# Conditioning rows of a decoder trunk through device memory instead of broadcast matmuls

## The reference

```python
c_act = jax.nn.silu(c)
for l in range(DEPTH):
    ada = (c_act @ ada_w[l] + ada_b[l])[:, None, :]
    sh1, sc1, g1, sh2, sc2, g2 = jnp.split(ada, 6, axis=-1)
    h = rms_norm(x, norm_mix_g[l]) * (1.0 + sc1) + sh1
    x = x + g1 * hybrid_mixer(h, ...)     # 8 heads: attention, pooling, recurrence, then w_out
    h = rms_norm(x, norm_ffn_g[l]) * (1.0 + sc2) + sh2
    x = x + g2 * peer_ffn(h, ...)         # 8 heads x 16 experts gathered for every token
return rms_norm(x, final_g)
```

## Time and profile before

| | |
|---|---|
| median of three runs | 2143.58 us |
| lowest, highest | 2141.44, 2143.63 us |
| span of the profiled execution | 2140.2 us |
| PE, PE weight loads | 1886.5 us (88%), 1105.7 us (52%) |
| DVE, ACT, POOL | 1485.8 (69%), 689.8 (32%), 629.5 us (29%) |
| moved by DMA | 713.13 MB, of it 536.90 MB gathers |

### The profile page before, as it was taken

One profiled execution on the slowest core, in us unless ns is written; L12 is line 12 of the kernel. 1 busy time (PEld: TensorE's weight loads), 2 busy tenths in 40 slices (PEclk: granted clock), 3 DMA queues, 4 the chain that ended last, 5 costly groups with the idle time before them and its releaser, 6 DMA issues.

```text
span 2140.2 us, 22226 instructions
## 1 busy us (share of the span) xinstructions
PE 1886.5 (88%) x6428; PEld 1105.7 (52%) x6428; DVE 1485.8 (69%) x4081; ACT 689.8 (32%) x1923; POOL 629.5 (29%) x608
## 2 busy tenths in 40 slices
PE   4999999989889889888799999999989889888777
PEld 3677777654334334333267777775434334334332
DVE  6587687686776766766646676677776766766774
ACT  1222232233333333333322232242333333333332
POOL 4000000044444444444400000002444444445442
PEclk9999999999999999999999999999999999999989
DMA  9855563389999999999986544336999999999997
GB/s 374 327 187 195 213 228 133 124 359 396 426 427 426 427 426 426 427 413 413 424 336 236 201 183 175 128 128 255 386 427 426 428 426 426 426 427 425 408 416 294
DMA packets 118819, 713.13 MB, mean 333 GB/s; under 512 B 13104, under 2 KB 17456, under 8 KB 51120
## 3 DMA queue, kind: packets, MB, share of 16 engines
q0 software_dynamic: 73728, 536.90, 60.0%
q1 hardware_dynamic: 44976, 174.97, 21.8%
HBM read 710.78 MB, written 1.05 MB: 333 GB/s over the span
## 4 chain that ended last, share of the span: by engine, by line
PE 57%; DMA 21%; DVE 12%; ACT 3%; issue 3%; POOL 2%; SPq 2%; DVEq 0%; POOLq 0%; ACTq 0%
DMA wall<-in_peer_uv,idx 19%; PE PS L1239 18%; PE PS L975 11%; PE PS L980 10%; DVE wall L1308 6%; PE PS L985 5%; PE PS L995 3%; POOL wall L634 2%; PE PS L1213 2%; ACT M L853 1%; PE PS L1022 1%; PE PS L1172 1%; ACT wgt L846 1%; DVE pos L1818 1%; PE PS L946 1%
## 5 line engine op out<-in xcount | busy, mean ns | idle before, releaser
L1239 PE MATMUL PS<-wall,M 128*128 128x512 f32 x2032 | 956.3, 621 | 207.1 <-ACT M L853 206.9
L1308 DVE CUSTOM_DVE_ANT_0 wall<-wall,tok 128x1024 f32<-128x1024 f32 x512 | 604.9, 1224 | 337.0 <-DMA wall<-in_peer_uv,idx 337.0
L634 POOL DMA_INDIRECT wall<-in_peer_uv,idx x512 | 570.5, 1114 | 699.9 <-PE PS L1239 512.0
L1239 PEld LDWEIGHTS PS<-wall,M 128*128 128x128 f32 x2032 | 387.7, 198 | 735.7 <-issue 414.4
L839 ACT ACTIVATE dg<-dg 128x2 f32<-128x2 f32 x254 | 51.7, 203 | 751.5 <-DVE dg L1308 751.5
L975 PE MATMUL PS<-hT,wall 128*128 128x256 f32 x1120 | 247.9, 381 | 1.7 <-DMA wall<-in_w_in 1.7
L975 PEld LDWEIGHTS PS<-hT,wall 128*128 128x128 f32 x1120 | 212.1, 190 | 31.4 <-ACT M L717 2.1
L576 POOL TENSOR_SCALAR rsb<-ms 128x4 f32<-128x4 f32 (+2 forms) x22 | 6.2, 284 | 749.8 <-DVE ms L1308 748.5
L980 PE MATMUL PS<-wall,hT 128*128 128x512 f32 x512 | 224.7, 593 | 0.2 <-ACT M L703 0.2
L853 ACT ACTIVATE M<-turn,wgt 128x128 f32<-128x128 f32 x508 | 176.2, 394 | 23.5
L980 PEld LDWEIGHTS PS<-wall,hT 128*128 128x128 f32 x512 | 96.3, 191 | 109.0 <-issue 108.3
(11 more groups left out here) (290 smaller groups left out, 1894.4 us busy)
## 6 DMA issues: line engine op xcount, KB each, us to landing
wall<-in_w_in SPq DMA_DIRECT2D x112, 704.0 KB, 9.6
braw<-in_ada_rows SPq DMA_DIRECT2D x72, 512.0 KB, 4.3
wall<-in_w_out SPq DMA_DIRECT2D x2, 4096.0 KB, 14.8
wall<-in_peer_uv,idx POOLq DMA_INDIRECT x512, 12.3
wall<-in_ada_rows SPq DMA_DIRECT2D x6, 1024.0 KB, 12.2
wall<-in_w_in SPq DMA_DIRECT2D x16, 384.0 KB, 10.1
mix<-in_peer_w_query SPq DMA_DIRECT2D x6, 1024.0 KB, 4.8
wall<-in_w_in SPq DMA_DIRECT2D x16, 320.0 KB, 8.9
```

What stands on the lines that cost most here:

```text
L634: nc.gpsimd.indirect_dma_start(out=pair_rows[b][s], out_offset=None, in_=uv_rows, in_offset=bass.IndirectOffsetOnAxis(ap=idx[i % 2][:, k:k ...
L1239: ins = mm(bank(B_ACC + 2 * t + hf), diag[:, b, s, :], pair_rows[b][s][:, D + hf * 512:D + (hf + 1) * 512], start=(i == FIRST_TILE[t] and ...
L1308: return v.tensor_tensor_reduce(out=o, in0=a, in1=b, scale=1.0, scalar=0.0, op0=ALU.mult, op1=ALU.add, accum_out=acc)
```

## The change

All 32 columns of a layer (24 of the looped heads, 8 of g2) are now kept in one array `acol` [128, 32], which `fold_cols` writes directly. In head 6's step PE turns the array with one matmul into 32 rows of 128 in PSUM, DVE copies them to `arow`, SP stores them to a 16 KB buffer in device memory, waits for the store, and reads them back with a broadcast over all 128 partitions into `ada` (16 KB a partition, 2 MB). `update_first` waits for that read. `block_row`, `block_out`, `gate_rows` and the copies of g2 are gone. The loop's constant `MIX_CHAIN` counts DVE's chained instructions, eight fewer for a pair of heads.

```diff
+ROWS = 4 * KC
-MIX_CHAIN = (160, 158)
+MIX_CHAIN = (152, 150)
-        acol = sb("acol", [P, 3 * KC])
+        acol = sb("acol", [P, ROWS])
+        arow = part(P)
+        bounce = nc.dram_tensor("bounce", (DEPTH, ROWS, P), F32, kind="Internal").ap()
@@ SP, after the loop of a layer
                 load_wq(l, 0, s_r[1])
+                sp.wait_ge(s_rowed, l + 1)
+                sp.dma_start(bounce[l], arow[0:ROWS, :]).then_inc(s_bounce, 16)
+                sp.wait_ge(s_bounce, 16 * (l + 1))
+                sp.dma_start(ada[:].rearrange("p a n -> p (a n)"), brow(bounce[l].rearrange("r n -> (r n)"), 4 * D)).then_inc(s_rows, 16)
                 sp.wait_ge(s_z, UNITS * HEADS * (l + 1))
                 load_wq(l, HEADS - 2, s_ahead)
@@ PE
-                def block_row(m, jm, p, dst):
-
-                    pe.wait_ge(s_col, m * 2 + (2 * H0 + G2_BLOCKS + p + 1))
-                    for i in range(2):
-                        mm(dst[:, i * P:(i + 1) * P], ccol[:, jm, p, i:i + 1].to_broadcast([P, P]), ident[:],
-                           start=True, stop=True)
+                def turn_columns():
+
+                    pe.wait_ge(s_col, (G2_BLOCKS + 2 * (HEADS - 2)) * (l + 1))
+                    mm(bank(B_S1)[0:ROWS, 384:512], acol[:], ident[:], start=True, stop=True)
@@ PE, step
-                    if rows:
-                        block_row(m, jm, 0, bank(B_S1)[:, 256:512])
+                    if isinstance(m, int):
+                        turn_columns()
                     attend(m, jm)
                     pe.wait_ge(s_AH, m + (H0 + 1))
-                    if rows:
-                        block_row(m, jm, 1, bank(B_O)[:, 256:512])
                     recur(m, jm)
@@ PE, first group of the experts
                         key_scores(1)
-                        gate_rows()
@@ DVE
-                def block_out(h, jm, p, src):
-
-                    ch(copy(acol[:, bass.ds(h * 4 + p * 2, 2)], ccol[:, jm, p, :]))
-                    ch(copy(ada[:].rearrange("p a n -> p (a n)")[:, bass.ds(h * 512 + p * 256, 256)], src))
-                        fold_cols(ecol[:, i, :], layer, j, 2).then_inc(s_col, 1)
+                        fold_cols(ecol[:, i, :], layer, j, 2, acol[:, 3 * KC + 2 * i:3 * KC + 2 * i + 2]).then_inc(s_col, 1)
-                        fold_cols(ccol[:, jm, p, :], l, j, 2).then_inc(s_col, 1)
+                        fold_cols(ccol[:, jm, p, :], l, j, 2, acol[:, bass.ds(h * 4 + p * 2, 2)]).then_inc(s_col, 1)
@@ DVE, step and last_pair
                     attended(h)
-                    block_out(h, j, 0, bank(B_S1)[:, 256:512])
                     forget(h + 1, 1 - j)
                     recurred(h)
-                    block_out(h, j, 1, bank(B_O)[:, 256:512])
                     recurred(h)
+                    copy(arow[0:ROWS, :], bank(B_S1)[0:ROWS, 384:512]).then_inc(s_rowed, 1)
                     squares()
@@ DVE, update_first and the first group of the experts
+                    dve.wait_ge(s_rows, 16 * (l + 1))
-                        dve.wait_ge(s_g2, l + 1)
-                        for hf in range(2):
-                            ch(copy(ada[:, 3, hf * 512:(hf + 1) * 512], bank(B_G2[hf])))
```

More of the change, by code:

```diff
@@ L76 @@
 B_H = ((B_S0, B_LA), (2, B_LB))
-B_G2 = (B_S0, B_O)
 B_TURN = (B_S0, B_LA, B_O)
@@ L308, in build @@
         s_pexp = sem("s_pexp")
-        s_g2 = sem("s_g2")
+        s_rowed, s_bounce, s_rows = sem("s_rowed"), sem("s_bounce"), sem("s_rows")
         s_six, s_seven, s_six_rest, s_y_rest = sem("s_six"), sem("s_seven"), sem("s_six_rest"), sem("s_y_rest")
@@ L1070, in step @@
                     jn = 1 - jm
-                    rows = not isinstance(m, int)
                     project(n, jn, 0)
@@ L1256, in expert_rows @@
                                 ins.then_inc((s_half, s_vacc)[hf], 1)
[L1258 to L1265, removed]
                 for g in range(LGROUPS):
@@ L1367, in constants, with fold_cols @@
                 ch.sync()
-            def fold_cols(a, l, j, n):
+            def fold_cols(a, l, j, n, to=None):
                 ch(v.tensor_tensor(a, a, bcol[:, l, bass.ds(j, n)], ALU.add))
                 ch.sync()
-                return v.tensor_tensor(a, a, gcol[:, l, bass.ds(j, n)], ALU.mult)
+                return v.tensor_tensor(a if to is None else to, a, gcol[:, l, bass.ds(j, n)], ALU.mult)
             def scale_rows(t):
```

## The result

The change makes the kernel slower: 2156.31 us against 2143.61 us for the kernel before, run beside it, a ratio of 1.0061 [1.0047, 1.0075]. The forecast was 2131.6 us, 0.56% less. The profiled execution of after took 2151.57 us, with a span of 2149.8 us.

The account below looks back on a forecast made before the run. PE's instruction stream bounds the mixer loops, DMA nearly all the expert stage. Span 2140.2 - 10.8 + 0.45 - 1.6 - 0 = 2128.2 us; with 3.4 around it, 2131.6 us, 0.56% less, range 2127.5 to 2137.

Parts of the forecast that it names:

- rival 1: Expert stage: removing the gate rows gains nothing, because DMA ends last or ACT is late; 2133.2 us, chance 22%.
- The loops, -10.8 us: Mixer loops: conditioning matmuls leave PE's stream, 0.90 us in each of twelve looped heads, paid back in full.
- rival 3: Mixer loops: PE meets a wait of 0.9 us a head, for AH or weights; 2142.4 us, no change, chance 5%.
- The turn, +0.45: Head 6's step: one added matmul before attend, 0.22 us a layer on PE's path; bounds nothing and 0.45.
- The round trip, 0: Head 6 to DVE's gate-row product: store and broadcast read, likely 11 us, worst 23, hidden under 35 us of cover.
- Rival 4: The round trip outlasts its 35 us cover, each further microsecond costing two; 2151.6 us at 45 us, chance 2%.
- The gate rows, -1.6 and 0: Expert stage's start: without sixteen matmul records (1.79 us) the second sum starts 1.6 us sooner in layer 0, 0 in layer 1.
- The earlier gathers find idle DMA: Layer 0's expert stage: DMA share 0.77 from 480 to 490 us leaves idle time for gathers that start sooner.
- The clock: Expert stages' starts: PE's clock left unchanged in the sum, +-3.1 us in the range; one fall more or fewer, chance 21%.

Follow-up runs that it names:

- e_before_off32: The kernel before with 32 unused bytes a partition in front of the SBUF tensor wall (target of mixer weights and gathers): 2165.73 us, ratio 1.0103.
- f_after_aligned: The changed kernel with 224 unused bytes a partition in front of wall, which then begins on a multiple of 256: 2128.25 us, ratio 0.9939 to before.
- a_again: The changed kernel run once more without an edit, beside the kernel before on the same chip: 2153.53 us, ratio 1.0048.
- l_thrice: f_after_aligned with the round trip made three times in series in each layer: 2132.36 us, ratio 0.9956 to before.
- n: f_after_aligned with 32 unused bytes behind wall, so wall stays aligned and the large tensors behind it lie 32 bytes off: 2132.22 us, ratio 0.9953 to before.
- j_all_aligned: The changed kernel with seven small tensors declared elsewhere, so every large SBUF tensor begins on a multiple of 256, without unused bytes: 2131.77 us, ratio 0.9948 to before.
- p_loop_only: The kernel before without the loops' conditioning matmuls and their copies, wall unmoved, g1 set to zero, no round trip: 2135.39 us, ratio 0.9962 to before.
- k_gate_back: f_after_aligned with the gate rows of g2 made by matmuls again in each layer: 2134.77 us, ratio 0.9963 to before.
- c_out: The changed kernel with the round trip through the first 32 KB of the output tensor and no internal tensor: 2153.85 us, ratio 1.0046 to before.

## Why the prediction was wrong

**The step that failed** is a term that the prediction's sum doesn't have. Its parts go through the matmuls, the copies, the round trip, the queue and the clock, and none takes a price for the declaration `acol = sb("acol", [P, ROWS])` or names it. It stands in the diff as plainly as the matmuls. Its price is the largest of all: e_before_off32 makes this edit's shift alone and takes 2165.73 - 2142.61 = 23.1 us; between f_after_aligned and a_again, with the change in both and each beside before on its own chip, the ratios differ by 0.0109, 23.3 us. The second half of the same failure is in rival 1, "DMA, whose bytes are fixed, is what ends last in the expert stage". The bytes are fixed. The rate was taken as fixed with them, and it fell from 427 to 417 GB/s. The size fits: the gathers' 8 KB packets together took 1278.9 us of 16 engines in before and 1299.2 in after, 20.3 us more, and the two expert stages are 9.9 and 9.7 us longer.

With `wall` aligned, four kernels that leave PE's stream as the change has it gave 0.9939 (f_after_aligned), 0.9956 (l), 0.9953 (n) and 0.9948 (j). The forecast was 2131.6/2143.58 = 0.9944. So the sum of the parts that were costed came out, and the error is the one part that was not. Some of the closeness is luck. The profiled executions of these four have spans 15.0, 12.7, 8.9 and 10.2 us under before's, where the sum had 12.0; in f_after_aligned the turn and a wait in layer 1 cost more than was taken, and the clock and a microsecond before head 2 gave more. The points, with the landmarks of f_after_aligned (head 2's step at 162.96, first gather 426.29, second sum 446.51, last sum 1071.02, output projection's end 1458.96, second sum of layer 1 at 1484.65, end 2125.2):

- **The loops, -10.8 us.** Right as a step: 164.28 to 207.37 is 43.09 us in after, against 43.98, and 43.09 in f_after_aligned too. In one of the twelve it isn't whole. Layer 1's first step in after is 1127.45 to 1171.41, still 43.96 us, since DVE waits for the rows of `ada_w` for 8.66 us inside it and PE then waits for DVE. In f_after_aligned that step is 1114.56 to 1157.96, 43.40 us. That is rival 3, with DMA as the late one, for 0.3 to 0.9 us in all. End to end p_loop_only gives 8.1 us [5.1, 10.9] for the loops, so the 10.8 stand as steps and are not shown to arrive in full.
- **The turn, +0.45.** Too small. Head 6's step is 340.08 to 383.69, 43.61 us, against 43.08: 0.53 us a layer, 1.06 in all, above the worst that was taken, 0.45 a layer. The matmul and the one behind it show as two pieces where the prediction took one of 0.22:

```profile
374.92 0.34 PE PS L1045 x2
375.25 0.42 PE PS L1050 x2
```

- **The round trip, 0.** Right, and its parts too: 1.4 and 7.3 us where 2 and 8 were taken, with 4 and 18 as the worst. DVE's product is still released by PE (at 410.85 in after). Rival 4, in which the round trip outlasts its cover, is refuted: one takes 8.7 us, and three in l_thrice still fit. The cover of 35 us measured as 32 to 33 (377.46 to 410.85 in after).
- **The gate rows, -1.6 and 0.** The sizes are right; in layer 0 the reason is only half of it. From the first gather to the second sum, before takes 455.60 - 433.78 = 21.8 us, after 20.2 and f_after_aligned 20.2. In layer 1, from the end of the output projection to the second sum, before takes 25.65 us (1474.28 to 1499.93), after 25.68 (1474.12 to 1499.80), f_after_aligned 25.69. ACT is late next, as said. What the prediction didn't say is that the rows cost something only behind a first sum at the lower clock. In the profiles of after and f_after_aligned that sum ran at the full clock (3.70 us), where the rows would have cost nothing (above), so their 1.6 us against before can't be told from a clock that didn't fall. That the rows' removal gives the time where the clock does fall is seen in j_all_aligned: 5.20 us for the first sum and still 20.2.
- **The earlier gathers find idle DMA.** From 480 to 490 us before moved 285 GB/s. After moves 411, which is all that it can at its rate, f_after_aligned 424 and k_gate_back 353; but c_out, with the schedule of after, moves 336. The profiled stage of f_after_aligned, 446.51 to 1071.02, is 1.7 us shorter than that of before.
- **The clock.** Layer 0's fall at the narrow matmuls is shorter, 5.24 us for the eight records in after and f_after_aligned (before 6.61), and layer 1 has a fall in after (5.24) that before (3.54) and f_after_aligned (3.54) don't have; k_gate_back had 6.39 in layer 0, l_thrice 3.54. It isn't the change that decides: a_again is after without an edit and had 6.41 where after had 5.24, and 5.22 for its first expert sum where after had 3.70. The same kernel falls or not from execution to execution, by up to 3 us at a place, and p_loop_only shows three slower places in one execution where the prediction's range allowed for one.

For one profile of each the differences between f_after_aligned and before add up: -7.5 up to the first gather (5.4 of the loop, less 0.5 for the turn, 1.4 of the clock, and about 1 before head 2 that no edit explains), -1.6 at the gate rows, -1.7 in the stage, -4.5 in the second mixer (five steps of 0.89, one of 0.58, less 0.5), +0.3 in the last stage: -15.0, the difference of the spans.

## What to carry to other kernels

Before costing the work that a change adds, list the on-chip tensors whose size or order it changes, and look where the targets of the large transfers come to lie: here a small tensor that grew by 32 bytes cost more than all the matmuls removed had saved. Where DMA runs full, keep these targets on multiples of 256 bytes a partition, by the order of the small tensors if no byte is to spare. And where a change is slower though every engine does less, compare the rate of a full DMA window in the first microseconds, ahead of what was rescheduled: it tells a cause in the layout from one in the schedule.

## What the runs showed of the hardware

**Large transfers into SBUF ran faster when their target began on a multiple of 256 bytes.** With `wall` 32 or 128 bytes behind one, the first loads moved 408 to 411 GB/s in every kernel, against 419 to 422 on a multiple; the gathers moved 415 to 420 against 422 to 427. The packets are equally many. From 14 to 20 us before moved 2.53 MB in packets of 4 KB, an engine's time of 16 x 6 us / 618 packets = 155 ns for each, and after 2.46 MB, 160 ns: 4 to 5 ns more. The mean duration of the gathers' packets of 8 KB is 312.0 to 313.1 ns in the eight kernels with `wall` on a multiple, 317.0 to 317.7 in the five with 32 bytes, and 316.3 with 128: 3 to 6 ns more.

The Trainium skill ("DMA: Bandwidth & Descriptors", "How a descriptor splits into AXI transactions") says that a descriptor is cut into pieces of 256 bytes that must start on multiples of 256, and that one which starts off such a multiple fetches from the boundary below. It doesn't say whether this holds for the written side; the runs here show a price on that side. Its size agrees with neither way of counting: one piece more would be an estimated 1/16 for 4 KB and 1/32 for 8 KB, against 2.9% (422 to 410 GB/s) and 1.6% (312.2 to 317.2 ns) measured, and by bytes fetched the offset of 128 should cost four times that of 32, while it measured the same in the first loads and no more in the gathers (316.3 against 317.0 to 317.7 ns). So of the three positions tried the multiple of 256 is the fast one, a multiple of 128 is not enough, and by what mechanism is open. Offsets other than 32 and 128 weren't tried, and neither was the reading side.

**Reading one short stretch by all partitions is cheap.** 2 MB read as 128 copies of 16 KB landed in 7.3 us, about 287 GB/s with the start included, and the 16 KB store before it in 1.4 us.
